# Up projections of 16 of 22 feature tiles as seven half-width products, with the low part of one block moved to VectorE

## What is computed

```python
h = _rmsnorm(x, g_ffn[l])
z = _dwconv_centred(h @ w_up[l], conv_w[l], conv_b[l])     # w_up 1024 x 5632
z_gate, z_val = jnp.split(z, [D_FF], axis=-1)              # D_FF = 2816
x = x + (jax.nn.silu(z_gate) * z_val) @ w_down[l]
```

## Time and profile before

| | |
|---|---|
| time, median of 3 runs (lowest, highest) | 1104.08 us (1103.99, 1104.28) |
| the profiled execution's span | 1102.4 us |
| what lies around the span (median less span) | 1.7 us |
| instructions | 16315 |
| TensorE / VectorE / ScalarE / GpSimd busy | 99% / 48% / 44% / 42% |
| DMA traffic | 108.79 MB, mean 99 GB/s |

### The profile page before, as it was taken

The page is one execution under the profiler, slowest core; times in us unless marked ns, Lnnn a source line. Parts: engine busy times, 40 slices in busy tenths (PEclk is TensorE's granted clock), DMA queues, the critical chain, the costliest instruction groups (busy, mean ns, idle before and its releaser), DMA issues.

```text
span 1102.4 us, 16315 instructions
## 1 busy us (share of the span) xinstructions
PE 1092.6 (99%) x5328; PEld 905.8 (82%) x5328; DVE 531.0 (48%) x816; ACT 484.7 (44%) x656; POOL 464.8 (42%) x202
## 2 busy tenths in 40 slices
PE   9999999999999999999999999999999999999997
PEld 7788888888888888888878888888888888888886
DVE  5726755655215551255536368456541355314545
ACT  7835444454225441344557344346432454313451
POOL 5334234344534443544634332435444444444450
PEclk9999999999999999999999999999999999999999
DMA  8222223232222222222522212222332322232222
GB/s 301 93 96 78 68 76 105 78 109 100 96 95 94 97 96 95 96 96 97 180 97 81 91 63 74 95 77 96 115 95 76 115 96 95 79 117 91 96 77 78
DMA packets 33607, 108.79 MB, mean 99 GB/s; under 512 B 3984, under 2 KB 6800, under 8 KB 33552
## 3 DMA queue, kind: packets, MB, share of 16 engines
q1 hardware_dynamic: 32848, 107.03, 29.2%
q10 hardware_dynamic: 704, 1.07, 0.3%
HBM read 105.98 MB, written 2.10 MB: 98 GB/s over the span
## 4 chain that ended last, share of the span: by engine, by line
PE 97%; DVE 1%; DMA 1%; ACT 0%; POOL 0%; SPq 0%; issue 0%; DVEq 0%
PE acc L1044 28%; PE acc L1045 28%; PE acc L1046 28%; PE acc L1170 3%; PE acc L1171 3%; PE acc L1172 3%; PE side L1140 1%; PE side L1258 1%; PE side L1242 1%; DMA x<-xT 1%; PE side L1248 1%; PE side L1221 1%; DVE arena L1019 1%; PE side L1201 1%; PE acc L1132 0%; PE acc L1121 0%
## 5 line engine op out<-in xcount | busy, mean ns | idle before, releaser
L339 POOL TENSOR_TENSOR w_lo<-w_raw,w_hi 128x1024 fp32r<-128x1024 f32 x188 | 453.4, 2416 | 600.6 <-ACT w_hi L348 600.6
L1044 PE MATMUL acc<-xg_hi,w_hi 128*128 128x512 f32 x864 | 338.8, 392 | 0.0
L1045 PE MATMUL acc<-xg_lo,w_hi 128*128 128x512 f32 x864 | 336.3, 389 | 0.0
L1046 PE MATMUL acc<-xg_hi,w_lo 128*128 128x512 f32 x864 | 336.2, 389 | 0.0
L348 ACT ACTIVATE w_hi<-w_raw 128x1024 fp32r<-128x1024 f32 x190 | 200.0, 1057 | 255.2 <-PE acc L1046 219.2
L1044 PEld LDWEIGHTS acc<-xg_hi,w_hi 128*128 128x128 f32 x864 | 162.2, 188 | 35.8 <-issue 2.0
L1046 PEld LDWEIGHTS acc<-xg_hi,w_lo 128*128 128x128 f32 x864 | 162.2, 188 | 33.9
L1045 PEld LDWEIGHTS acc<-xg_lo,w_hi 128*128 128x128 f32 x864 | 162.2, 188 | 33.5 <-issue 0.5
L1044 PE MATMUL acc<-feat_hi,w_hi 128*128 128x512 f32 (+1 forms) x492 | 188.9, 384 | 0.0
L1045 PE MATMUL acc<-feat_lo,w_hi 128*128 128x512 f32 (+1 forms) x492 | 188.8, 384 | 0.0
L1046 PE MATMUL acc<-feat_hi,w_lo 128*128 128x512 f32 (+1 forms) x492 | 188.8, 384 | 0.0
(11 more groups left out here) (131 smaller groups left out, 803.2 us busy)
## 6 DMA issues: line engine op xcount, KB each, us to landing
w_raw<-slabs SPq DMA_DIRECT2D x190, 512.0 KB, 3.3
outT<-arena SPq DMA_DIRECT2D x7, 256.0 KB, 2.3
ln_sb<-ln_gb SPq DMA_DIRECT2D x2, 512.0 KB, 7.7
w_raw<-slabs SPq DMA_DIRECT2D x4, 128.0 KB, 4.6
x<-xT ACTq DMA_DIRECT2D x2, 256.0 KB, 4.6
x<-xT SPq DMA_DIRECT2D x2, 256.0 KB, 5.9
x<-xT ACTq DMA_DIRECT2D x1, 512.0 KB, 7.2
w_raw<-slabs SPq DMA_DIRECT2D x2, 256.0 KB, 6.9
```

The source lines that it names most:

```text
L339: pool.tensor_tensor(w_lo[:, w], w_raw[:, w], w_hi[:, w].bitcast(F32), ALU.subtract).then_inc(lo_done, 1)
L1044: pe.matmul(out, wh, ah, start=first, stop=False)
L1045: pe.matmul(out, wh, al, start=False, stop=False)
L1046: return pe.matmul(out, wl, ah, start=False, stop=last)
```

## The change

The parts become 6, 8 and 8 tiles. The first works as before. In the other two (16 tiles, 8 quads a layer) a quad is multiplied by the Strassen-Winograd scheme. The operands are seen as 2x2 blocks: the quad's weights (blocks A11, A12, A21, A22; even and odd channel blocks against the two feature tiles) and the activations (channel blocks against the halves of 256 positions). Seven products replace eight. Each takes one 128x1024 slab-sized unit of weights and a half-width activation:

- weights: A11, A12, A22 as loaded; S1 = A21 + A22, S3 and S4 by DMAs that add to what lies in the destination, issued by GpSimd; S2 = S1 + A11 by VectorE (signs are moved to the activations);
- activations: T1 to T4, made once a layer beside the first part (`combine`, `t_low` on VectorE, `copy_e12`, `t_high` on ScalarE);
- outputs: several products add up in one bank. ScalarE copies four intermediate sums out (P5 after product S1, P1 after A11, U2 after S2, U3 after S3), and VectorE makes the four quarter sums C11, C12, C21, C22 from banks and copies. Then come scaling, taps, Silu and gate as before, in a new order.

A quad loads four slabs and reads two of them a second time for the adding DMAs. Of the seven units a quad, GpSimd makes six low parts, and VectorE that of A22. The last part now has eight blocks, not six, in its down tiles. Scratch for T, the raw blocks and the copies is taken from buffers of the mixing stage. The core of the diff, in this order: GpSimd's transfers and its order in a quad (`low_quad`); ScalarE's (`quad_step`); VectorE's low part of A22, its order in a quad (`convolve`, `quad_step`; KP = 4 quads a part); TensorE's `product` (H = 256) and its order (`up_products`). In `raw0`, `raw1`, `raw2` lie A11, A21 and A12 of a quad.

```diff
+def add_s1(L, p, s):
+    pool.wait_ge(a21_loaded[s % 2], 16 * ((L * QUADS + p * KP + s) // 2 + 1))
+    pool.dma_start(raw1[s % 2], block_of(L * NS + first_slab(p, s) + 3),
+                   accum_op=ALU.add).then_inc(s1_added[s % 2], 16)
+def add_s3(L, p, s):
+    low_done(L * NU + first_unit(p, s) + A11_)
+    pool.wait_ge(s2_done, L * QUADS + p * KP + s + 1)
+    pool.dma_start(raw0[s % 2], block_of(L * NS + first_slab(p, s) + 1),
+                   accum_op=ALU.add).then_inc(s3_added[s % 2], 16)
+def add_s4(L, p, s):
+    low_done(L * NU + first_unit(p, s) + A12_)
+    pool.dma_start(raw2[s % 2], s2_raw, accum_op=ALU.add).then_inc(s4_added[s % 2], 16)
+def low_quad(L, p, s):
+    n = L * NU + first_unit(p, s)
+    low(n + S1_, raw1[s % 2])
+    low(n + A11_, raw0[s % 2])
+    add_s3(L, p, s)
+    if s < KP - 1:
+        add_s1(L, p, s + 1)
+    low(n + A12_, raw2[s % 2])
+    add_s4(L, p, s)
+    low(n + S2_, s2_raw)
+    low_done(n + A22_)
+    low(n + S3_, raw0[s % 2])
+    low(n + S4_, raw2[s % 2])
...
+def quad_step(p, s):
+    if s:
+        centre(p, s - 1, 1)
+    high_s2(p, s)
+    if s:
+        centre(p, s - 1, 0)
+    copy(p, s, S1_, 2 + s % 2, p5_copy)
+    high_a22(p, s)
+    if s:
+        centre(p, s - 1, 2)
+        silu(p, s - 1, 0)
+        centre(p, s - 1, 3)
+    copy(p, s, A11_, 1, p1_copy)
+    high_s3(p, s)
+    if s:
+        silu(p, s - 1, 1)
+        feat_high(p, s - 1, 0)
+    high_s4(p, s)
+    if s:
+        feat_high(p, s - 1, 1)
+        act.wait_ge(c12_added, quad_at(p, s))
+    copy(p, s, S2_, 1, u2_copy)
+    if s < KP - 1:
+        high_s1(p, s + 1)
+        high_a11(p, s + 1)
+    else:
+        high_down(p, 0)
+        high_down(p, 1)
+    copy(p, s, S3_, 1, u3_copy)
+    if s < KP - 1:
+        high_a12(p, s + 1)
+    else:
+        high_down(p, 2)
...
+def low_a22(p, s):
...
+    dve.wait_ge(hi_done, L * NU + (unit + 1))
+    dve.wait_ge(lo_done, L * NU + (unit + RING))
+    dve.tensor_tensor(w_lo[:, w], raw(3), w_hi[:, w].bitcast(F32), ALU.subtract).then_inc(lo_done, 1)
...
+def convolve(p, s, between):
+    add_c12(p, s)
+    scale(p, s, 0)
+    taps(p, s, 1)
+    scale(p, s, 2)
+    taps(p, s, 0)
+    if s < KP - 1:
+        low_a22(p, s + 1)
+    scale(p, s, 3)
+    taps(p, s, 2)
+    between()
+    gate(p, s, 0)
+    taps(p, s, 3)
+    quad_low(p, s, 0)
+    gate(p, s, 1)
+    quad_low(p, s, 1)
+def quad_step(p, s):
+    if s:
+        convolve(p, s - 1, (lambda: add_s2(p, s + 1)) if s < KP - 1 else (lambda: None))
+    else:
+        low_a22(p, 0)
+        add_s2(p, 1)
+    add_c11(p, s)
+    add_c22(p, s)
+    add_c21(p, s)
+    scale(p, s, 1)
...
+def product(bank, unit, moving, first):
+    slab_wait(unit)
+    for k in range(KP):
+        for r in range(2):
+            a = (unit % RING) * SLAB + r * (SLAB // 2) + k * P
+            xh, xl = moving(k)
+            out = acc[bank][:, r * H:(r + 1) * H]
+            pe.matmul(out, w_hi[:, a:a + P], xh, start=(first and k == 0 and r == 0), stop=False,
+                      skip_group_check=True)
+            pe.matmul(out, w_hi[:, a:a + P], xl, start=False, stop=False, skip_group_check=True)
+            last = pe.matmul(out, w_lo[:, a:a + P], xh, start=False, stop=(k == KP - 1),
+                             skip_group_check=True)
+    last.then_inc(acc_ready, 1)
...
+def up_products(p, s):
+    n = first_unit(p, s)
+    quads = L * QUADS + p * KP + s
+    own, other = 2 + s % 2, 3 - s % 2
+    def free(added, tile):
+        if s:
+            pe.wait_ge(added, quads)
+        else:
+            pe.wait_ge(x_done, L * NX + RING + (p + 1) * KT + tile + 1)
+    def has_copied(n_copies):
+        pe.wait_ge(copied, quads * 4 + n_copies)
+    free(c21_added, 6)
+    if p == 0 and s == 0:
+        pe.wait_ge(t1_ready, L + 1)
+        pe.wait_ge(t_ready, (L + 1) * KP)
+    product(own, n + S1_, t1, True)
+    free(c22_added, 5)
+    product(1, n + A11_, b11, True)
+    free(c11_added, 4)
+    product(0, n + A12_, b21, True)
+    has_copied(2)
+    product(1, n + S2_, t2, False)
+    free(c12_added, 7)
+    product(other, n + A22_, t4, True)
+    has_copied(3)
+    product(1, n + S3_, t3, False)
+    product(own, n + S4_, b22, False)
```

More of the change, by code:

```diff
@@ L334, in _, with low @@
                                    ALU.subtract).then_inc(lo_done, 1)
[L335 to L340, removed]
+            def low(unit, source):
+                j = unit % RING
+                w = slice(j * SLAB, (j + 1) * SLAB)
+                pool.wait_ge(hi_done, unit + 1)
+                pool.tensor_tensor(w_lo[:, w], source, w_hi[:, w].bitcast(F32), ALU.subtract).then_inc(lo_done, 1)
@@ new lines, in _ @@
+            for L in range(DEPTH):
+                at = L * NU
+                low_slabs(at + (RING if L == 0 else 0), at + N_DOWN + RING)
+                for p in range(FULL_PARTS):
+                    n = at + first_unit(p)
+                    low(n - 4, raw(0))
+                    low(n - 3, raw(1))
+                    low(n - 2, raw(2))
+                    add_s1(L, p, 0)
+                    low(n - 1, raw(3))
+                    for s in range(KP):
+                        low_quad(L, p, s)
+                    down = at + first_unit(p, KP)
+                    low_slabs(down, down + RING)
+                low_slabs(at + NU - RING, at + NU)
@@ L640, in _ @@
+                for p in range(FULL_PARTS):
+                    first_highs(p)
+                    for s in range(KP):
+                        quad_step(p, s)
+                    last_step(p)
+                    if p < FULL_PARTS - 1:
+                        for m in range(RING, KT):
+                            high_down(p, m)
                 act.activation(ln_std[:, 0:1], ones[:, 0:1], ACT.Sqrt)
@@ L966, in _, with quad_at, halves @@
-                for q in range(LAST_TILES // 2):
-                    up_quad(N_LAST + q * RING, FULL_PARTS * KT + 2 * q, lambda b: featT(True, 2 * q + b),
-                            lambda b: featT(False, 2 * q + b))
+                        if b == 0:
+                            combine(k)
+                    feat_low(tile + 1, tile + 1, 1)
+                    t_low(k)
+                def quad_at(p, s):
+                    return L * QUADS + (p * KP + s)
+                def halves(bank):
+                    return bank.rearrange("p (r s) -> p r s", r=2)
```

520 lines of the change are left out of this document (404 added, 116 removed).

## The result

The changed kernel takes 1111.5 us (median; 1111.0 to 1113.4), the kernel before 1104.05 beside it: a ratio of 1.0071, 95% interval 1.0056 to 1.0085. It is 7.4 us slower. TensorE saves what it was to save, and waits more than that away.

What follows compares the result with a forecast made beforehand. TensorE, 99% busy, was taken to bound the kernel. The terms -25.6 + 0.2 (half tiles) + 26.7 (ring) + 1.0 (first part) gave +2.3 us on the median 1104.08: 1106.4 us, range 1090 to 1128.

Steps and rivals of the forecast that it cites:

- TensorE's saving: Products on TensorE: a quad takes 20.16 us instead of 21.76, over 16 quads 25.6 us less.
- Rival 4: TensorE's 256-column matmuls don't keep 120 ns in long stretches; each 0.01 us costs 27 us; 0.05 together with another rival.
- The issue cost: GpSimd's time d to issue one DMA: 1.0 us, with eight d's in a part, 32 in all.
- Rival 1: GpSimd's DMA issue is cheap, d from 0.33 to 0.8: 1091 to 1101 us, chance 0.30.
- rival 2: Issue or accumulation is dear: d of 1.5, or S4's transfer landing after 5.9 us; 1114 to 1150 us, chance 0.20.
- The landing of the accumulating transfers: Time for GpSimd's adding DMAs to land: 4 to 6 us, against 3.3 for a plain load.
- the sign that I had named as wrong: VectorE waiting for a DMA before S2's sum, which would point to rival 2.
- The ring: Waits round ScalarE, GpSimd and VectorE, 23.6 us between U2 copies in a middle quad; costs 26.7 us over four parts.
- The second quad's term: The ring's loss in each part's second quad, where it starts earlier: 1.3 us.
- The product that waits: TensorE's idle place: S3 behind U2's copy in second and third quads, S2 behind P1's copy in the fourth.
- A22's low part on VectorE: VectorE's new pass over 128x1024: about 1.22 us, waiting for GpSimd's low part of S2 through a shared semaphore.
- First part: Ordinary quads with added combining passes on VectorE, slowed beside GpSimd: 0.5 us a layer, +1.0 in all.

Runs made afterwards that it cites:

- e8: Changed kernel with S1 lacking its addend A21, so one accumulating transfer fewer per quad (output changes): 1104.2 us, ratio 1.0003 to the kernel before.
- e1: Changed kernel with A22's low part made by GpSimd again instead of VectorE: 1119.2 us, ratio 1.0131 to the kernel before.
- e9: Changed kernel with A22's low part on GpSimd and the add of the next S2 last in VectorE's convolution: 1089.8 us.
- e12: Against a 1105.6 us kernel (changed kernel, own semaphore for A22's low part, next S2's add last): VectorE's fourth scaling put ahead of that low part; 1088.9 us.
- e2: Changed kernel with a semaphore of its own for A22's low part on VectorE, which no longer waits for GpSimd's count: 1110.15 us.
- e11: Against a 1085.8 us kernel (own semaphore for A22's low part, next S2's add last, ScalarE's copies first): last token combination behind the first down adds; 1083.3 us.
- e7: Changed kernel with five small products on TensorE before its wait for the copy of P1, in second and third quads: 1115.1 us.
- e4: Changed kernel with ScalarE's copies of P1 and U2 ahead of the centre tap and feature high part that wait for VectorE: 1099.1 us.

## Why the prediction was right, and where it wasn't

The forecast was 1106.4 us with a range of 1090 to 1128, slower with 0.46; measured 1111.5.

- **TensorE's saving**, -25.6: right. The first quads take 20.16 us, the steps are 120 ns, and half tiles cost 0.2. Rival 4 is out. The figures of the Trainium skill (TensorE: Matmul & The Clock Gate, Back-to-back issue gap), which would have given 38, were off by as much as the earlier trace rows said. They are that section's gap of an isolated matmul; for a stream of weight loads and matmuls it gives about 131 ns at 512 columns, and the 226.7 ns here are further still from that.
- **The issue cost**, 1.0: right, 0.88 and 1.19, the two back to back overlapping by 0.3, and 0.30 before an issue that waits for GpSimd's own pass. GpSimd's stretch from the start of S1's low part to the end of S2's is 12.9 us (304.13 to 317.04, 328.05 to 340.95), and the sum had 9.9 + 3.0. e8 shows that it counts. Rival 1 is out. Its prices were off anyway: by its own count, 32 d's, the loss at 0.7 falls by 9.6 us, which gives 1097 and not 1099, at 0.35 with the floors about 1088 and not 1092; and rival 2's d of 1.5 adds 16, not 17.
- **The landing of the accumulating transfers**, 4 to 6: S3's 5.4, S4's 6.0 with 7.1 at most, S1's 7.3 in the median. So S4's passed rival 2's point of 5.9, and the sign that I had named as wrong, VectorE waiting for a DMA before S2's sum, did appear: 4.9 us, of which 3.3 are in first quads and harmless. But it wasn't a rival to the ring, as I put it: it was the second wait in the same queue, hidden by the first. e1 shows it, and e9 takes it away.
- **The ring**, +26.7: closed, as forecast, by the very members that I named, at 23.85 us from copy to copy where the sum had 23.6, and found at 30.8. The quads of the first part take 20.16, 23.75, 23.64 and 21.47 us (rows above), where I had 20.2, 21.5, 23.5 and 22.2. Over all four parts the second quads lose 10.4 us (I had 5.2), the third 14.2 (13.6), the fourth 6.2 (8.0). The second quad's term, 1.3, was too small: it came to 3.6 in the first part, of which 1.6 are steps at the lower clock. S2's low part ended there 6.9 us into the quad and not 6.0, since GpSimd began S1's 14.1 us into the first quad (304.13; I had 13.5), and I had left out its 0.3 us waits on its own results here. And I had left out, for this quad, the way over the fourth centre and the copy of P1: by the fourth quad's steps that copy would have ended at 9.5 us, where product S2 could start at 8.64. That the total came out as near owes something to luck, as the fourth quads were off the other way.
- **The product that waits**: half wrong. I put it before S3, behind the copy of U2, in the second and third quads, and before S2, behind the copy of P1, in the fourth. Twelve gaps, 0.66 to 2.9 us, are before S2; those before S3 are 0.64 us or less. The chain over the fourth centre, which I read for the fourth quad alone, is what TensorE meets in every quad but the first; e12 shows it, with 16.7 us for an exchange of two instructions. The wait before S3 stayed short since product S2 was late already: in the third quad of the first part the copy of U2 ends at 350.87, about 1 us before product S3 starts, and S2 had started 1.89 us late.
- **A22's low part on VectorE, 1.22**: right at 1.226 in the changed kernel, because it waits for GpSimd first. I gave its two passes no price for the shared port, though I priced it for the first part. With the wait away it is 2.5 (e2).
- **First part**, +1.0: mis-sized; 2.8. Not the six tiles' combining, whose chain was short enough, but the last combination ahead of the first down adds (e11).
- **The clock**: I had none of it. It fell four times, and by e7 mostly where it cost nothing.

What the experiments don't settle: why some waits of 2 us let the clock fall and others don't, and how e1's 7.7 us divide. The gaps behind the held add (3.3 us in its trace) are only its visible part, since the add runs slower beside GpSimd in the third quads too (1.7 to 3.0 us).

## What to carry to other kernels

Where a scheme trades matmuls for passes on other engines, look at the order inside each engine's queue before you look at its load: here the places of two copies of 0.6 us and of one add, and a count that isn't shared, were worth 26 us, and no engine beside TensorE was over 61% busy. Waits in one queue stand behind each other, so taking one away shows the next; of the edits here one alone gained 1.4 us, one nothing, one lost 7.7, and the last two together gained 21.7. Here a copy that frees a bank belonged ahead of whatever waited for another engine (e4).

## What the runs showed of the hardware

- A VectorE pass with two inputs in SBUF can be held through several GpSimd passes: 9.85 us for a 1.23 us add, where each GpSimd pass starts 0.3 us before the one before it ends. Where the next one starts only as the last ends, it got in after one (2.45 us in e9). The Trainium skill (SBUF — State Buffer, SBUF: two separate sides) has the shared pair of ports as an exclusive lock for a whole instruction, taken by whoever starts first; the trace agrees for one pass (2.5 us in e2), and shows that up to four in a row can hold VectorE off.
- A DMA that GpSimd issues costs its queue 0.88 to 1.19 us, and an accumulating transfer of 512 KB lands 5.4 to 7.3 us after its issue (medians by line), where plain loads of that size took 3.3 before, and 3.5 to 4.9 beside those transfers in the changed kernel (medians by destination).
- TensorE's granted clock can fall to its lower level after a wait of 1.9 us (1.89 us, then a mean of 0.58 over 3.4 us), and some 1.1 us of products inside the wait kept it up in all eight places where they stood, in one trace.
